# Forgetting attention: scores in three passes of high and low parts, and another order at the end of a head

## What is computed

```python
def _fox_branch(q, k, v, z, f_logit, b_f):          # 8 heads of 128, blocks of 128 queries
    log_f = jax.nn.log_sigmoid(f_logit + b_f)
    f_cum = jnp.cumsum(log_f, axis=1)
    def one_block(args):
        logits = jnp.einsum("bhqd,bhkd->bhqk", qi, k) * scale
        logits = logits + fi[..., :, None] - f_cum[..., None, :]
        logits = jnp.where(pi[:, None] >= kpos[None, :], logits, -jnp.inf)
        probs = jax.nn.softmax(logits, axis=-1)
        return jnp.einsum("bhqk,bhkd->bhqd", probs, v)
    ...
    return o * jax.nn.silu(z)
```

## Time and profile before

| what | value |
|---|---|
| median of 3 runs | 1934.16 us (1931.32 to 1938.37) |
| the profiled execution's own time | 1931.09 us |
| its span, first to last instruction | 1929.5 us |
| TensorE busy | 1878.4 us, 97% |
| VectorE busy | 1179.9 us, 61% |
| ScalarE busy | 749.9 us, 39% |
| share of the chain that ended last, TensorE | 83% |
| mean granted TensorE clock | 0.995 |

### The profile page before, as it was taken

One profiled execution on the slowest core, in us unless ns is written; L12 is line 12 of the kernel. 1 busy time (PEld: TensorE's weight loads), 2 busy tenths in 40 slices (PEclk: granted clock), 3 DMA queues, 4 the chain that ended last, 5 costly groups with the idle time before them and its releaser, 6 DMA issues.

```text
span 1929.5 us, 26490 instructions
## 1 busy us (share of the span) xinstructions
PE 1878.4 (97%) x9556; PEld 1523.8 (79%) x9556; DVE 1179.9 (61%) x1541; ACT 749.9 (39%) x1145; POOL 176.2 (9%) x324
## 2 busy tenths in 40 slices
PE   7999999999999999999999999999999999999998
PEld 4787887787787887888888887878777878888786
DVE  6675544455457777767777444468344446766976
ACT  5424344235224444444444433242233335331423
POOL 1000110110000001000000000032100002110200
PEclk9999999999999999999999999999999999999999
DMA  9541754644332111222122843433301111211402
GB/s 356 148 79 33 121 96 111 109 125 153 127 109 55 58 53 58 63 77 72 45 68 99 285 139 98 120 120 86 114 23 47 35 33 36 74 33 31 139 31 98
DMA packets 169298, 181.21 MB, mean 94 GB/s; under 512 B 11010, under 2 KB 143546, under 8 KB 168314
## 3 DMA queue, kind: packets, MB, share of 16 engines
q1 hardware_dynamic: 155168, 130.69, 21.5%
q0 software_dynamic: 13760, 49.30, 11.5%
q10 hardware_dynamic: 282, 0.09, 0.0%
HBM read 139.56 MB, written 40.50 MB: 93 GB/s over the span
## 4 chain that ended last, share of the span: by engine, by line
PE 83%; DVE 5%; DMA 4%; ACT 2%; issue 2%; PEld 1%; DVEq 1%; SPq 1%; ACTq 0%; PEldq 0%; POOL 0%; POOLq 0%
PE acc L302 22%; PE acc L285 22%; PE acc L1607 15%; PE work L1615 3%; PE acc L1632 3%; PE acc L3119 3%; PE acc L2578 2%; PE work L1624 2%; PE acc L1021 2%; PE work L2559 1%; PEld acc L285 1%; PE work L2568 1%; PE acc L3426 1%; DMA dskip<-in_d_skip 1%; DVE conv_out L845 1%
## 5 line engine op out<-in xcount | busy, mean ns | idle before, releaser
L302 PE MATMUL acc<-ha_hi,w_hi 128*128 128x512 f32 x640 | 257.9, 403 | 2.9 <-DVE nxt L2375 1.6
L302 PE MATMUL acc<-ha_hi,w_lo 128*128 128x512 f32 x640 | 250.2, 391 | 0.0
L302 PE MATMUL acc<-ha_lo,w_hi 128*128 128x512 f32 x640 | 249.5, 390 | 0.0
L285 PE MATMUL acc<-ha_hi,w_hi 128*128 128x512 f32 x592 | 187.0, 397 | 7.7 <-ACT ha_hi L562 1.9
L285 PE MATMUL acc<-ha_lo,w_hi 128*128 128x512 f32 x592 | 185.6, 395 | 3.2 <-DVE ha_lo L723 1.6
L285 PE MATMUL acc<-ha_hi,w_lo 128*128 128x512 f32 x592 | 183.8, 392 | 0.0
L261 ACT ACTIVATE w_hi<-w_raw 128x1024 fp32r<-128x1024 f32 x96 | 101.2, 1054 | 179.2 <-PE acc L302 80.8
L265 DVE TENSOR_TENSOR w_lo<-w_raw,w_hi 128x1024 fp32r<-128x1024 f32 x96 | 117.7, 1226 | 51.4 <-ACT w_hi L261 49.0
L302 PEld LDWEIGHTS acc<-ha_hi,w_hi 128*128 128x128 f32 x640 | 120.4, 188 | 27.7 <-issue 3.7
L302 PEld LDWEIGHTS acc<-ha_hi,w_lo 128*128 128x128 f32 x640 | 120.1, 188 | 26.3
L285 PEld LDWEIGHTS acc<-ha_hi,w_hi 128*128 128x128 f32 x592 | 110.8, 190 | 35.8 <-issue 10.5
(11 more groups left out here) (517 smaller groups left out, 3615.9 us busy)
## 6 DMA issues: line engine op xcount, KB each, us to landing
w_raw<-in_w_in SPq DMA_DIRECT2D x99, 512.0 KB, 4.1
acs_bc<-acs_scr POOLq DMA_DIRECT2D x8, 1024.0 KB, 15.8
w_raw<-in_w_out SPq DMA_DIRECT2D x11, 512.0 KB, 4.0
x_tok<-in_x SPq DMA_DIRECT2D x8, 512.0 KB, 7.1
w_scale<-in_w_ada SPq DMA_DIRECT2D x8, 512.0 KB, 9.7
w_shift<-in_w_ada SPq DMA_DIRECT2D x8, 512.0 KB, 9.0
xt_scr<-xt SPq DMA_DIRECT2D x1, 4096.0 KB, 13.3
w_ada_g<-in_w_ada SPq DMA_DIRECT2D x8, 512.0 KB, 12.7
```

Source lines behind the costliest of these rows:

```text
L285: mm = pe.matmul(acc[:, n % 2, h * HALF:(h + 1) * HALF], w[:, n % 2, k, :], x[:, k, h * HALF:(h + 1) * HALF], start=(k == 0 and i == 0), s ...
L302: mm = pe.matmul(acc[:, 0, half * HALF:(half + 1) * HALF], w[:, n % 2, k, :], x[:, k, half * HALF:(half + 1) * HALF], start=(k == 0 and i ...
```

## The change

q and k of a head are now kept as high and low parts (`q_hi`, `k_hi`, `q_lo`, `k_lo`), made by GpSimd with two casts and two subtractions, and each piece of scores is three fp32r passes instead of one fp32 product. No piece has fewer than 256 columns: where a tile has one tile of keys, two are computed, and from tile 4 on the pieces are cut anew (tile 4 as 384 + 256 instead of 512 + 128). The low part of k takes room in SBUF, so `y_head`, `y_hi` and `y_lo` are gone: the gated result is written over `silu_za`, and it is rounded, subtracted and saved in two halves, the first before the head's last tile is weighed, through one buffer `y_hi_half` that lies in the space of the turned weights. At the end of a head on TensorE, fill(12) goes ahead of turn(7), and fill(13) ahead of values(7).

```diff
         def fox_chunks(t):
             first = sum((v + BANK_TILES) // BANK_TILES for v in range(t))
-            return [(first + i, a, min(a + BANK_TILES, t + 1)) for i, a in enumerate(range(0, t + 1, BANK_TILES))]
+            cuts = [0, t + 1] if t < BANK_TILES else [0, min(BANK_TILES, t - 1), t + 1]
+            return [(first + i, a, b) for i, (a, b) in enumerate(zip(cuts, cuts[1:]))]
...
             def save_y(h):
-                wait_here(sp, x_lo_done, LO_SPLITS[5] + h + 1)
-                for i in range(2):
-                    sp.dma_start(row(y_hi_scr, h)[:, i * HALF:(i + 1) * HALF], y_hi[i][:, :].bitcast(F32)).then_inc(y_saved, 16)
-                sp.dma_start(row(y_lo_scr, h), y_lo[:, :].bitcast(F32)).then_inc(y_saved, 16)
+                for i, lo in enumerate((y_lo_1st, y_lo_2nd)):
+                    s = slice(i * HALF, (i + 1) * HALF)
+                    wait_here(sp, x_lo_done, LO_SPLITS[5] + 2 * h + i + 1)
+                    sp.dma_start(row(y_hi_scr, h)[:, s], y_hi_half[:, :].bitcast(F32)).then_inc(y_saved, 16)
+                    sp.dma_start(row(y_lo_scr, h)[:, s], lo[:, :].bitcast(F32)).then_inc(y_saved, 16)
...
                 wait_here(pool, pair_added, 10 * h + 5)
-                pool.tensor_copy(q_t[:, :], next_tiles[0][:, :])
-                pool.tensor_copy(k_t[:, :], next_tiles[1][:, :])
+                pool.tensor_copy(q_hi[:, :], next_tiles[0][:, :])
+                pool.tensor_copy(k_hi[:, :], next_tiles[1][:, :])
+                pool.drain()
+                pool.tensor_tensor(q_lo[:, :], next_tiles[0][:, :], q_hi[:, :].bitcast(F32), ALU.subtract)
+                pool.tensor_tensor(k_lo[:, :], next_tiles[1][:, :], k_hi[:, :].bitcast(F32), ALU.subtract)
                 pool.drain().then_inc(taken, 1)
...
                         if c >= 2:
                             pe.wait_ge(logits_done, FC * h + c - 1)
-                        pe.matmul(work[:, c % 2, 0:(b - a) * P], q_t[:, t * P:(t + 1) * P], k_t[:, a * P:b * P],
-                                  start=True, stop=True).then_inc(qk_done, 1)
+                        w = max(b - a, 2) * P
+                        for i, (q, k) in enumerate(((q_hi, k_hi), (q_hi, k_lo), (q_lo, k_hi))):
+                            mm = pe.matmul(work[:, c % 2, 0:w], q[:, t * P:(t + 1) * P], k[:, a * P:a * P + w],
+                                           start=(i == 0), stop=(i == 2))
+                        mm.then_inc(qk_done, 1)
...
-                for t in range(5, NT):
+                for t in range(5, NT - 1):
                     turn_probs(t)
                     fill(t + 5)
                     weigh_values(t)
+                fill(12)
+                turn_probs(NT - 1)
                 fill(13)
+                weigh_values(NT - 1)
...
                 act.wait_ge(pair_added, 10 * h + 10)
+                act.wait_ge(x_lo_done, LO_SPLITS[5] + 2 * h)
                 act.activation(silu_za[:, :], next_tiles[3][:, :], ACT.Silu)
...
                 act.wait_ge(x_lo_done, T_BASE + 4)
+                act.wait_ge(y_saved, Y_SAVED + 64 * h)
                 copies(0)
...
                 else:
+                    act.wait_ge(y_gated, 2 * h + 3)
+                    act.wait_ge(pv_done, NT * h + 7)
+                    act.activation(y_hi_half[:, :], silu_za[:, T1], ACT.Copy).then_inc(x_hi_done, 1)
                     hi(14)
                     hi(15)
-                act.wait_ge(y_gated, 2 * h + 4)
...
-                    act.wait_ge(y_saved, Y_SAVED + 48 * h)
-                    for i in range(2):
-                        e = act.activation(y_hi[i][:, :], y_head[:, i * HALF:(i + 1) * HALF], ACT.Copy)
-                    e.then_inc(x_hi_done, 1)
                     hi(16)
+                    act.wait_ge(y_gated, 2 * h + 4)
+                    act.wait_ge(y_saved, Y_SAVED + 32 + 64 * h)
+                    act.activation(y_hi_half[:, :], silu_za[:, T2], ACT.Copy).then_inc(x_hi_done, 1)
...
+                def y_low(half, dst):
+                    dve.wait_ge(x_hi_done, SPLITS[5] + 2 * h + half + 1)
+                    dve.tensor_tensor(dst[:, :], silu_za[:, half * HALF:(half + 1) * HALF], y_hi_half[:, :].bitcast(F32),
+                                      ALU.subtract).then_inc(x_lo_done, 1)
```

More of the change, by code:

```diff
@@ L1381, in build @@
         ar = arena()
-        q_t = ar("q_t", [P, T])
-        k_t = ar("k_t", [P, T])
+        q_hi = ar("q_hi", [P, T], F32R)
+        k_hi = ar("k_hi", [P, T], F32R)
+        q_lo = ar("q_lo", [P, T], F32R)
         v_tok = ar("v_tok", [P, NT, FOX_D])
+        at_gated = ar.at
         silu_za = ar("silu_za", [P, T])
@@ L1387, in build @@
         prob = ar("prob", [P, 2, T])
+        at_split = ar.at
         prob_t = ar("prob_t", [P, 2, NT, P])
-        at_y = ar.at
-        y_head = ar("y_head", [P, T])
-        y_lo = Region(at_y, arena_end)("y_lo5", [P, T], F32R)
+        y_lo_1st = Region(at_gated, arena_end)("y_lo_1st", [P, HALF], F32R)
+        y_split = Region(at_split, arena_end)
+        y_hi_half = y_split("y_hi_half", [P, HALF], F32R)
+        y_lo_2nd = y_split("y_lo_2nd", [P, HALF], F32R)
         next_v = ar("next_v", [P, T])
@@ L1396, in build @@
         row_inv = ar("row_inv", [P, 2])
-        y_hi = [ar("y_hi5", [P, HALF], F32R)]
+        kept5 = ar("kept5", [P, HALF])
         KH = KT // 2
@@ L1557, in sp_5 @@
             product_done(9)
-            sp.wait_ge(y_saved, Y_SAVED + 48 * last)
+            sp.wait_ge(y_saved, Y_SAVED + 64 * last)
             sp.dma_start(ya_hi[:, 0:4, :].bitcast(F32), y_hi_scr[:, 0:4, :]).then_inc(y_back, 16)
@@ L1789, in head @@
                     split_hi(act, N_MIX2)
[L1790 removed]
+                    act.wait_ge(y_gated, 2 * h + 4)
+                    act.activation(ya_hi[:, FOX_HEADS - 1, :], silu_za[:, :], ACT.Copy).then_inc(x_hi_done, 2)
+                else:
+                    act.wait_ge(y_gated, 2 * h + 3)
+                    act.wait_ge(pv_done, NT * h + 7)
+                    act.activation(y_hi_half[:, :], silu_za[:, T1], ACT.Copy).then_inc(x_hi_done, 1)
                     hi(14)
                     hi(15)
[L1793 to L1800 removed]
                     hi(16)
+                    act.wait_ge(y_gated, 2 * h + 4)
+                    act.wait_ge(y_saved, Y_SAVED + 32 + 64 * h)
+                    act.activation(y_hi_half[:, :], silu_za[:, T2], ACT.Copy).then_inc(x_hi_done, 1)
             with act.Fori(0, FOX_HEADS // 2 - 1) as j:
@@ L1947, in head @@
                 dve.wait_ge(za_ready, h + 1)
-                dve.wait_ge(y_saved, Y_SAVED + 48 * h)
                 gate(0)
                 add_kept5(1)
+                if not last:
+                    y_low(0, y_lo_1st)
                 read(12)
@@ L1956, in head @@
                     lo(14)
+                    lo(15)
+                read(13)
+                if not last:
+                    weight_sums_in_place(dve)
                 gate(1)
                 if not last:
-                    lo(15)
-                    weight_sums_in_place(dve)
-                read(13)
-                dve.wait_ge(x_hi_done, SPLITS[5] + h + 1)
+                    lo(16)
+                    y_low(1, y_lo_2nd)
                 if last:
+                    dve.wait_ge(x_hi_done, SPLITS[5] + 2 * h + 2)
                     dve.wait_ge(late_saved[0], LATE_SAVED)
-                    dve.tensor_tensor(ya_lo[:, FOX_HEADS - 1, :], y_head[:, :], ya_hi[:, FOX_HEADS - 1, :].bitcast(F32), ALU.subtract
-                                      ).then_inc(x_lo_done, 1)
-                else:
-                    for i in range(2):
-                        s = slice(i * HALF, (i + 1) * HALF)
-                        dve.tensor_tensor(y_lo[:, s], y_head[:, s], y_hi[i][:, :].bitcast(F32), ALU.subtract)
-                    dve.drain().then_inc(x_lo_done, 1)
-                    lo(16)
+                    dve.tensor_tensor(ya_lo[:, FOX_HEADS - 1, :], silu_za[:, :], ya_hi[:, FOX_HEADS - 1, :].bitcast(F32), ALU.subtract
+                                      ).then_inc(x_lo_done, 2)
             with dve.Fori(0, FOX_HEADS // 2 - 1) as j:
```

20 lines of the change are left out of this document (8 added, 12 removed).

## The result

The changed kernel's median is 1939.69 us (5 runs, 1938.5 to 1944.64), beside 1932.36 us of the kernel before in the same series: ratio 1.0044, 95% interval 1.0029 to 1.0059. The profiled execution has a span of 1937.4 us, 7.9 more than before.

A forecast was written before the change was run, and what follows sets the result against it. TensorE, busy 97% of the span, was taken as the bound: -10.4 + 9.0 + 4.0 + 0.9 = +3.5 us on the profiled 1931.09 gives 1934.6; forecast median 1937 us, range 1927 to 1943.

The forecast's parts named there:

- The three-pass scores: Scores(3) to (7) on TensorE: 5.15 us a head instead of 6.45, 10.4 us less over 8 heads.
- Gate(1) late: VectorE at a head's end: gate(1) comes 4.8 us later in the head, delaying ScalarE's second rounding and keep(0).
- Heads 1, 3, 5, 6: At fill(2): 1.8 us of new idle time in each of heads 1, 3, 5, 6, 7, 9.0 us together.
- the half microsecond that the prediction named as a sign: Sign in the changed profile: the undisturbed heads are half a microsecond longer than before.
- the end of the stage: Before the output product: ScalarE gives back both banks later, behind values(7), gate(1) and a rounding; 0.9 us more.
- Heads 2 and 4: Passages where VectorE's loop jumps back, with one more ScalarE table load: fill(2) 2.0 us later each, 4.0 us together.
- about 0.3 to be back in step: TensorE after a wait at fill(2): starts 0.04 us after release and needs about 0.3 us to regain its pace.
- What is late disappears in head 0's wait for keep(0): Start of head 0: lateness from GpSimd's casts and subtractions is absorbed by fill(2)'s wait for keep(0); no cost.
- GpSimd "nothing": GpSimd's casts and subtractions, 5.9 to 7.8 us a head, stay hidden under over 12 us of TensorE work.
- Saves of y: Rival: the first half's save is late, so the second rounding and keep(0) wait; 1941 us, slower; 14%.
- narrow passes bound by weights: Rival: a 256-column score pass takes 0.19 us, bound by its weight load; +3.4 us, 1940.5 us, slower; 9%.
- The first rival: The saving comes through: ScalarE reaches keep(0) by 7.6 us after a head's first score, waits vanish; 1925 us, faster; 17%.

The follow-up runs named there:

- version 5: Changed kernel with fp32 score products in place of the three passes, all else kept: 1948.31 us, ratio 1.0078 against the kernel before.
- Version 8: Kernel before with only gate(1) moved on VectorE behind lo(15), the sums in place and read(13): 1943.02 us, ratio 1.0058 against the kernel before.
- version 6: Changed kernel with gate(1) moved on VectorE to right behind lo(15), ahead of read(13): 1929.19 us, ratio 0.9984 against the kernel before.
- Version 4: Changed kernel without GpSimd's two subtractions per head, low parts set to zero once, passes kept: 1937.16 us, ratio 1.0032 against the kernel before.
- version 3: Changed kernel with TensorE's old order at a head's end (turn(7), fill(12), values(7), fill(13)): 1941.63 us, ratio 1.0057 against the kernel before.
- version 7: Changed kernel with gate(1) right behind lo(15) and read(12) ahead of y_low(0) on VectorE: 1927.93 us, ratio 0.9974 against the kernel before.
- version 1: Changed kernel with keep(0) and hi(3) moved on ScalarE ahead of the copy of v: 1930.36 us, ratio 0.9993 against the kernel before.
- 9: Version 7 with keep(0) and hi(3) ahead of the copy of v and keep(3) ahead of exps(2) on ScalarE: 1924.42 us, ratio 0.996.
- version 10: Version 7 with keep(0) and hi(3) ahead of the copy of v on ScalarE, keep(3) not moved: 1927.29 us, ratio 0.9977.

## Why the prediction was right, and where not

The median, 1939.69 us, lies inside the range, 2.7 above the forecast. The path was right: gate(1) late, keep(0) late, waits at fill(2) that outweigh the faster scores. The size was not: the sum was +3.5 us where the first pass of the output product moved by 9.25 and the medians by 7.3. The level that I started from, 1934.16, stood 1.8 above the median of before in this series, which hid part of the difference; that is luck. (By the sum's own terms the forecast would have been 1937.7 and not 1937.) I gave "within 0.3%" the greatest chance and "slower" 0.27; with 1.0044, interval from 1.0029, it came out slower, at the edge of the 0.3%.

- **The three-pass scores**: 10.4 us forecast, 9.8 by the pieces, 8.1 by version 5. A piece of 512 columns takes the 0.69 us that it should; the pieces cut in two cost 0.01 to 0.03 more.
- **Gate(1) late**: forecast at 3.48 us after the head's first score, measured 3.64; the second rounding 4.29 and 4.45; keep(0)'s end 9.10 and 9.20. The forecast counts from the chain's starts, 0.17 us later than the timeline's, and with that the three agree within 0.1 us. Version 8 shows that this place is enough for the loss, version 6 that the loss goes with it.
- **Heads 1, 3, 5, 6**: 1.8 us each forecast. Their lengths rose by 0.54 to 0.72, the half microsecond that the prediction named as a sign, and with the 1.22 that the scores save that is 1.76 to 1.94 us: idle times of 1.42 (three times) and 1.70, and 0.2 to 0.4 to be back in step. Head 7: 1.21 + 1.22 = 2.43 for the wait (1.17) and the end of the stage (0.86 more idle time) together, where 1.8 + 0.9 were forecast.
- **Heads 2 and 4**: 2.0 each forecast. Head 2: 0.92 + 1.22 = 2.14. Head 4: 2.60 + 1.22 = 3.82, of which 1.4 are passes at half the pace (the next point).
- **After a wait "about 0.3 to be back in step"**: this step failed, in two heads. Behind the waits of heads 0 and 4, 8 and 7 passes went every 0.42 to 0.43 us instead of 0.227: 8 x 0.2 = 1.6 and 7 x 0.2 = 1.4 us, 3.0 in all. This is of one profiled execution; another can have more or fewer of them.
- **"What is late disappears in head 0's wait for keep(0), which hangs on ScalarE's own work. Nothing."** This failed too. GpSimd's casts began at 592.62 and its second subtraction ended at 600.27, in the prediction's own bounds, and TensorE's first score went 0.1 us later, 0.92 us later than before. The wait for keep(0) did not absorb that; it grew, from 1.56 to 2.23 us, since keep(0) itself started 1.59 us later (609.85, before 608.26). VectorE's and ScalarE's timelines at the start of the stage show by what:

```profile
595.26 2.76 DVE L1510 TENSOR_TENSOR w_sum<-w_raw 128x512 f32<-128x512 f32 x1
598.15 3.28 DVE L1499 TENSOR_TENSOR w_lo<-w_raw,w_hi 128x512 fp32r<-128x512 f32 x2
```

```profile
602.98 1.92 ACT L1706 ACTIVATE ha_hi<-quad 128x2048 fp32r<-128x2048 f32 x1 [1.43 <-DVEq L1867]
```

Beside GpSimd's subtractions the sum takes 2.76 us (before 0.69) and the two low parts 3.28 (before 1.29). ScalarE's last split ahead of the heads (`ha_hi`) waits 1.43 us for the sums behind them, where it had waited for nothing (it started at 601.40), and the copy of v, silu and keep(0) follow it back to back. The sentence had left out that GpSimd slows VectorE, and that ScalarE waits for VectorE there. Version 4, without the subtractions, has neither delay.
- **GpSimd "nothing"** held inside the heads (version 4), for the reason given: three fills and more lie over it. The contention with VectorE wasn't in the working; inside the heads TensorE's new order kept it off the path (version 3).
- **Saves of y, narrow passes bound by weights**: neither rival shows. The first rival named the point from which it decides, gate(1) 1.5 to 2 us earlier; version 6 has gate(1) 1.4 us after the head's first score instead of 3.64, and in heads 1, 3 and 5 the saving came through (1.1 of 1.22 us each); over all heads it is 3.0 us of 9.8, head 0's slow passes (1.6) included.

Together: -9.8, +7.3 (heads 1, 3, 5, 6), +2.4 (head 7), +4.6 (heads 2 and 4 without slow passes), +0.8 (head 0's longer wait), +3.0 (slow passes), +0.9 (late start): 9.2 us. What makes the clock fall in head 4 and not in head 2, whose waits are as long, is open.

## What to carry to other kernels

A change that frees one engine can be paid for by the order of the others: list what stands behind each new wait, as here y_low(0) on VectorE, and follow it to the release that the freed engine needs next. Put the step on which another engine's whole list hangs ahead of work that nobody waits for; here one line in another place is worth about 11 us, slow passes included, no less than the faster scores. And when a wait goes, ask what the moved steps now stand ahead of, since the next release in the list (keep(3) here) can take its place.

## What the runs showed of the hardware

**Half clock behind short waits.** TensorE was busy up to 850.5 us, idle for 1.59 us, busy for 0.8, idle for 1.32, and then went at a granted clock of 0.50 up to 857.3. Nearly the same idle times in head 2 (1.67 and 1.26) left it at 1.00, and in version 3 it was head 2, with 0.27 and 1.26 us, that fell to 0.50, and not head 4 with 0.20 and 1.33. 2.23 us of idle time in head 0 came with slow passes in the changed kernel and in version 6 and without them in version 7, and the idle time of some 2.1 us at the end of the stage came with them in versions 1, 5, 6, 9 and 10 (in version 1 the clock is 0.50 from 1078.5 to 1081.5), outside the heads' sum, and without them in the changed kernel, 4 and 7. So behind idle times of 1.26 to 2.23 us there were slow passes, worth 1.4 to 1.6 us, in some heads and executions and not in others; what decides is open. It is in the scatter of the medians too: the twelve executions of version 10 go from 1925.56 us at a mean clock of 0.997 to 1932.07 at 0.992. The Trainium skill, "TensorE: Matmul & The Clock Gate", section "Back-to-back issue gap", gives columns / 1.2 ns from start to start at the lower level, 427 ns for 512; the trace agrees (854.82 to 855.24 to 855.67).

**GpSimd and VectorE.** While GpSimd subtracts (two inputs in SBUF, 2.6 to 2.8 us for 1,024 elements), VectorE's subtractions with two SBUF inputs took 4.07 us for two instead of 1.85, and the scaling of 1,024 elements by a column 2.62 instead of 0.75. In head 3 both end 0.54 to 0.55 us after the GpSimd subtraction beside them (773.85 and 773.31; 776.62 and 776.07), and the sum at the start of the stage does too (598.02 and 597.47): as if VectorE's operation were held until GpSimd's had ended, rather than slowed, which no run tests. The copies of GpSimd do it as well: the first sum of the stage took 1.40 us beside them in the kernel before, where 0.69 is usual. No VectorE operation with an input in PSUM lies beside a subtraction in the changed kernel's trace. The Trainium skill, "GPSIMD Engine Reference", section "Specifications", says that its SBUF interfaces are shared with VectorE, with contention where a VectorE instruction has two SBUF inputs or runs in a 2-port mode. The trace agrees for the subtractions (4.07 against 1.85); the scaling has one such input, and no run shows in which mode it runs.
